# Output panels held back for the layer norm: two tiles finished first, and ScalarE rounding three weight panels

## The reference

```python
for layer in range(2):                      # first block; the second has no cross attention
    x = layer_norm(ALPHA * x + mixer(x) @ w_out, g0, b0)
    x = layer_norm(ALPHA * x + memory_cross_attention(x, mem, wq, wkv, wo), g1, b1)
    x = layer_norm(ALPHA * x + swiglu(x, w_gu, w_down), g2, b2)
```

## Time and profile before

| | us |
|---|---|
| median of 3 runs (3221.38 to 3228.93) | 3225.34 |
| the profiled execution | 3220.99 |
| its span, first to last instruction | 3219.2 |
| PE busy | 3025.5 |
| POOL busy | 1751.4 |
| DVE busy | 921.4 |
| ACT busy | 645.0 |

### The profile page before, as it was taken

How to read it: one execution, slowest core, us unless ns; L and a number is a source line. 1 busy time by engine, 2 the same in 40 slices (tenths; PEclk the granted TensorE clock), 3 DMA queues, 4 the chain that set the end, 5 groups by cost and what they waited for, 6 DMA issues and landing times.

```text
span 3219.2 us, 35940 instructions
## 1 busy us (share of the span) xinstructions
PE 3025.5 (94%) x15048; PEld 2511.7 (78%) x15048; DVE 921.4 (29%) x1470; ACT 645.0 (20%) x1330; POOL 1751.4 (54%) x1472
## 2 busy tenths in 40 slices
PE   7889999999999897999999999899999998999998
PEld 6776778888887666788888887878888886788887
DVE  3535402311023295023100221833110056530102
ACT  1224212211010162122100121452010032420100
POOL 5540383566665503836666656423666665556664
PEclk9999999999999998999999999989999999899999
DMA  4221241322223202412322232002323222033232
GB/s 143 71 74 40 70 143 50 105 92 98 99 87 104 66 1 66 144 53 92 105 92 94 90 112 92 1 1 81 103 92 104 93 98 79 14 100 97 92 105 79
DMA packets 182498, 267.15 MB, mean 83 GB/s; under 512 B 6592, under 2 KB 145984, under 8 KB 182336
## 3 DMA queue, kind: packets, MB, share of 16 engines
q1 hardware_dynamic: 174240, 243.28, 22.9%
q10 hardware_dynamic: 8096, 21.56, 2.0%
HBM read 262.73 MB, written 2.10 MB: 82 GB/s over the span
## 4 chain that ended last, share of the span: by engine, by line
PE 79%; DVE 14%; POOL 3%; issue 1%; ACT 1%; DMA 1%; ACTq 0%; DVEq 0%; POOLq 0%
PE PS L464 23%; PE PS L465 23%; PE PS L466 23%; PE PS L785 3%; POOL wlo L2084 2%; DVE PS L665 2%; DVE x_row L660 1%; PE PS L771 1%; DVE nmx L1434 1%; PE PS L1324 1%; DVE xT_lo L566 1%; DVE x_row L672 1%; PE PS L917 1%; POOL whi L2079 1%; PE PS L549 1%
## 5 line engine op out<-in xcount | busy, mean ns | idle before, releaser
L2079 POOL TENSOR_SCALAR whi<-raw 128x1024 fp32r<-128x1024 f32 x460 | 485.7, 1076 | 1336.2 <-DMA raw<-ffn_w 270.0
L2084 POOL TENSOR_TENSOR wlo<-raw,whi 128x512 fp32r<-128x512 f32 x920 | 1188.5, 1328 | 0.0
L464 PE MATMUL PS<-xT_hi,whi 128*128 128x512 f32 (+1 forms) x2304 | 856.0, 372 | 41.4 <-DVE xT_lo L566 29.1
L465 PE MATMUL PS<-xT_lo,whi 128*128 128x512 f32 (+1 forms) x2304 | 848.7, 368 | 0.0
L466 PE MATMUL PS<-xT_hi,wlo 128*128 128x512 f32 (+1 forms) x2304 | 848.5, 368 | 0.0
L464 PEld LDWEIGHTS PS<-xT_hi,whi 128*128 128x128 f32 x2304 | 441.6, 192 | 118.1 <-DVE xT_lo L566 32.4
L465 PEld LDWEIGHTS PS<-xT_lo,whi 128*128 128x128 f32 x2304 | 441.6, 192 | 71.5 <-issue 2.4
L466 PEld LDWEIGHTS PS<-xT_hi,wlo 128*128 128x128 f32 x2304 | 441.4, 192 | 70.1
L464 PE MATMUL PS<-whi,xT_hi 128*128 128x512 f32 x672 | 264.5, 394 | 23.6 <-ACT a_pre L1025 16.3
L960 DVE TENSOR_TENSOR htmp<-sil,PS 128x512 f32<-128x512 f32 x88 | 56.5, 683 | 804.0 <-ACT sil L945 804.0
L464 PE MATMUL PS<-whi,h_hi 128*128 128x512 f32 x704 | 274.1, 389 | 0.0
(11 more groups left out here) (360 smaller groups left out, 3218.5 us busy)
## 6 DMA issues: line engine op xcount, KB each, us to landing
raw<-ffn_w SPq DMA_DIRECT2D x66, 1024.0 KB, 5.0
raw<-ffn_w_gu SPq DMA_DIRECT2D x44, 1024.0 KB, 5.1
raw<-ffn_w_down SPq DMA_DIRECT2D x22, 1024.0 KB, 5.0
raw<-mem_wkv SPq DMA_DIRECT2D x16, 1024.0 KB, 5.4
raw<-even_w_in SPq DMA_DIRECT2D x14, 1024.0 KB, 5.2
raw<-ev_w_in SPq DMA_DIRECT2D x14, 1024.0 KB, 5.3
raw<-odd_w_in SPq DMA_DIRECT2D x12, 1024.0 KB, 5.1
raw<-od_w_in SPq DMA_DIRECT2D x10, 1024.0 KB, 5.0
```

Source lines behind the costliest of these rows:

```text
L464: pe.matmul(o, lhs[0], rhs[0], start=start, stop=False, skip_group_check=True)
L465: pe.matmul(o, lhs[0], rhs[1], start=False, stop=False, skip_group_check=True)
L2079: pool.tensor_scalar(whi[b][:, cs], raw[b][:, cs], 1.0, 1.0, ALU.mult, ALU.mult).then_inc(panel_hi, 1)
L2084: m = pool.tensor_tensor(wlo[b][:, cs], raw[b][:, cs], whi[b][:, cs].bitcast(F32), ALU.subtract)
```

## The change

Three panels are held instead of two. In each of the ten stages PE adds N-2, N-1 and N to tiles 0 and 1 first, then does tiles 2 and 3, with the transposes of tiles 0 and 1 in between. The orders of ACT and DVE around the norm follow: both tiles' transposes are copied before tile 2 is centred. The hi halves of the panels N, N+1 and N+2 are made by ACT (`act_cut`), not by POOL; POOL keeps their lo halves and waits for ACT through `panel_hi_act`.

```diff
         for st in stages:
...
+            last_panel.append(len(panels) + nk // 2 - 1)
+        cut_panels = [n + k for n in last_panel for k in range(3) if n + k < len(panels)]
+
+        def act_cut(act, n):
+            b = n % NB
+            act.wait_ge(panel_loaded[b], 16 * (n // NB + 1))
+            for q in range(2):
+                cs = slice(1024 * q, 1024 * q + 1024)
+                act.activation(whi[b][:, cs], raw[b][:, cs], ACT.Copy).then_inc(panel_hi_act, 1)
...
-            for i in range(nk // 2 - 2):
+            for i in range(nk // 2 - 3):
...
             def finish(t):
-                add(1, t).then_inc(y_ready, 1)
-            two = next_panel(pe)
-            for t in (0, 1, 2):
-                add(0, t)
-            two += next_panel(pe)
+                add(2, t).then_inc(y_ready, 1)
+            three = next_panel(pe)
+            add(0, 0)
+            add(0, 1)
+            three += next_panel(pe)
+            add(1, 0)
+            add(1, 1)
+            three += next_panel(pe)
             finish(0)
             finish(1)
+            add(0, 2)
             add(0, 3).then_inc(panel_used, 1)
-            finish(2)
             if head:
                 turn(0)
+            add(1, 2)
+            if head:
+                turn(1)
+            add(1, 3).then_inc(panel_used, 1)
+            finish(2)
             finish(3)
             if head:
-                turn(1)
                 head(pe, lambda: (turn(2), turn(3)))
...
+            last = last_panel[at_stage[0]]
+            act_cut(act, last)
             deviation(0)
             deviation(1)
             if head:
                 act_turn(act, xT_hi, 0, KD, 0, 0)
+                act_turn(act, xT_hi, 0, KD, 2, 1)
+                act_cut(act, last + 1)
             deviation(2)
             if head:
-                act_turn(act, xT_hi, 0, KD, 2, 1)
+                act_cut(act, last + 2)
             deviation(3)
...
             finish(0)
             finish(1)
-            centre(2)
             if head:
                 dve_turn(dve, xT_hi, xT_lo, 0, KD, 0, 0)
-            else:
+                dve_turn(dve, xT_hi, xT_lo, 0, KD, 2, 1)
+            centre(2)
+            if not head:
                 finish(2)
             centre(3)
             if head:
-                dve_turn(dve, xT_hi, xT_lo, 0, KD, 2, 1)
                 finish(2)
             finish(3)
...
-                for q in range(2):
+                by_act = n in cut_panels
+                for q in range(0 if by_act else 2):
                     cs = slice(1024 * q, 1024 * q + 1024)
                     pool.tensor_scalar(whi[b][:, cs], raw[b][:, cs], 1.0, 1.0, ALU.mult, ALU.mult).then_inc(panel_hi, 1)
...
+                    if q % 2 == 0 and by_act:
+                        pool.wait_ge(panel_hi_act, 2 * cut_panels.index(n) + q // 2 + 1)
```

More of the change, by code:

```diff
@@ L267, in build @@
         panel_hi = sem("panel_hi")
+        panel_hi_act = sem("panel_hi_act")
         panel_split = sem("panel_split")
@@ L375, in build @@
         pool_at = []
+        last_panel = []
         for st in stages:
@@ L569, in dve_turn @@
             m.then_inc(lo_ready, 1)
+        cut_panels = [n + k for n in last_panel for k in range(3) if n + k < len(panels)]
+        def act_cut(act, n):
+            assert n in cut_panels
+            b = n % NB
[3 more added lines that the diff above has]
+                act.activation(whi[b][:, cs], raw[b][:, cs], ACT.Copy).then_inc(panel_hi_act, 1)
         n_ln = {"pe": 0, "act": 0, "dve": 0}
@@ L596, in add @@
                 ts = slice(128 * t, 128 * t + 128)
-                h, lo = two[i]
+                h, lo = three[i]
                 for c in range(2):
@@ L600, in add @@
                         cs = slice(1024 * k + 512 * c, 1024 * k + 512 * c + 512)
-                        kk = nk - 4 + 2 * i + k
+                        kk = nk - 6 + 2 * i + k
                         m = product(pe, PS[:, 2 * t + c, :], (lh[:, kk, ts], ll[:, kk, ts]),
-                                    (h[:, cs], lo[:, cs]), False, i == 1 and k == 1)
+                                    (h[:, cs], lo[:, cs]), False, i == 2 and k == 1)
                 return m
             def finish(t):
-                add(1, t).then_inc(y_ready, 1)
-            two = next_panel(pe)
-            for t in (0, 1, 2):
-                add(0, t)
-            two += next_panel(pe)
+                add(2, t).then_inc(y_ready, 1)
[6 more added lines that the diff above has]
+            three += next_panel(pe)
             finish(0)
             finish(1)
+            add(0, 2)
             add(0, 3).then_inc(panel_used, 1)
-            finish(2)
             if head:
                 turn(0)
+            add(1, 2)
[3 more added lines that the diff above has]
+            finish(2)
             finish(3)
             if head:
-                turn(1)
                 head(pe, lambda: (turn(2), turn(3)))
@@ L2081, in _ @@
                     cs = slice(512 * q, 512 * q + 512)
-                    if q % 2 == 0:
-                        pool.wait_ge(panel_hi, 2 * n + q // 2 + 1)
+                    if q % 2 == 0 and by_act:
+                        pool.wait_ge(panel_hi_act, 2 * cut_panels.index(n) + q // 2 + 1)
+                    elif q % 2 == 0:
+                        pool.wait_ge(panel_hi, 2 * (n - sum(k < n for k in cut_panels)) + q // 2 + 1)
                     m = pool.tensor_tensor(wlo[b][:, cs], raw[b][:, cs], whi[b][:, cs].bitcast(F32), ALU.subtract)
```

## The result

The changed kernel takes 3198.47 us (median of 4, 3197.73 to 3204.66) against 3224.67 for the one before in the same comparison: ratio 0.9922, 95% interval 0.9905 to 0.9939, 26 us faster. Forecast were 3193 (range 3177 to 3216), 32 us faster. The profiled execution's span is 3196.8.

What follows compares the result with a forecast made beforehand. PE's waits were taken to bound the kernel, 4.1 to 4.5 us per norm for xT_lo. Terms 28.0 + 5.2 - 0.4 = 33 us off the profiled 3220.99 give 3188; counted from the median 3225.3, 3193 (range 3177 to 3216).

Steps and rivals of the forecast that it cites:

- the three waits: PE's new waits at a norm: for N 0.6 us, N+1 0.1 at the head's start, N+2 1.7 48 matmuls later.
- The copies on ScalarE: ACT's copy of the first 1024 columns of a panel's hi half, taken as 1.1 us before POOL can start.
- POOL beside L665: POOL's lo half of N+2 takes 5.96 us, not 5.05, because tile 3's centring on DVE runs beside it.
- The seven norms before an FFN or mixer: Transposes of tiles 2 and 3 start 3.6 us earlier per norm: 25.2, with the longer slow stretches 28.0 us gained.
- three longer stretches: Three of the seven norms had a longer 1.2 GHz stretch at the head; its going gives 1.2 + 1.0 + 0.6 us more.
- rival A: The new wait for N+2 brings a slow-clock stretch each time, 1.7 us at nine norms, 15 us lost: 3208; chance 0.18.
- The two cross attentions: At the norms before them POOL's chain through the memory's panels counts and ends 2.6 us earlier, twice: 5.2 us gained.
- The last norm: Nothing follows it; N's wait of 0.6 us is paid and 0.2 comes back: a loss of 0.4 us.
- Rival C: With a fast ACT copy and POOL not slowed, N+2 is ready in time, 12 us more gained: 3181; chance 0.13.
- B: Slower: as rival A, but N's wait also brings a slow stretch and N+2's a double one: 3238; chance 0.05.
- D: Tile 0's row and N+1 miss their slack and waits inside the mixers take back half the gain: 3209 to 3220; chance 0.12.
- the slack that was forecast: Tile 0's row is ready 0.8 us before PE transposes that tile in the second norm, so PE does not wait.

Runs made afterwards that it cites:

- the last kernel: Two panels held with tiles 0 and 1 first, as in the run with two held, but ScalarE makes N+2's hi half alone, in four pieces: 3173.23 us, ratio 0.9846.

## Why the prediction was right

**That the panels take the norm's place: right.** The wait for the lo parts went at every norm; the forecast named the three waits and put them at 0.6, 0.1 and 1.7 us. Measured in the second norm: 0.53, none and 1.74, the last between 1.73 and 1.74 at all nine norms. The two one-sided runs (order alone, ScalarE alone) show that with three panels held both parts are needed, which the forecast had only in its arithmetic.

**The copies on ScalarE: right in size.** 1.1 us was taken between bounds of 0.63 and 1.27; the group's mean is 1.05.

```profile
L584 ACT ACTIVATE whi<-raw 128x1024 fp32r<-128x1024 f32 x56 | 56.1, 1051 | 447.1 <-DMA raw<-ffn_w_down 178.6 <-DMA raw<-ffn_w 178.5 <-DMA raw<-mem_wo 29.8
```

The estimate from the Trainium skill's page "ScalarE: Activation LUTs" (section "What ACT_TABLE_LOAD costs"), 1.04 us, agrees.

**POOL beside L665: right.** 5.96 us was taken for N+2's lo half, 6.00 measured. That is 0.96 more than the 5.04 of an undisturbed lo half, so the 0.9 of the forecast held and not the 1.29 that it set beside it; N+1's lo half wasn't disturbed at all (5.04). What was not in the sum is that DVE pays too: its L691 took 2.19 us there instead of 1.29. This is off the path: tile 3's row ended at 585.25 and the transposes of tiles 2 and 3 start at 588.99.

**The seven norms before an FFN or mixer: the term was 28.0 and gave 22.3.** This is the term that was mis-sized. (By the forecast's own figures the first of its three longer stretches gives 1.1, not 1.2.) Two things were off. (a) 0.3 to 0.6 us a norm, but for the one before the odd mixer, in the steps between N and the head. At the second norm, from N's load to the transposes of tiles 2 and 3 the forecast had 45.15 us (540.55 to 585.7), measured 45.73 (543.26 to 588.99). Of this 0.6, 0.1 is that N is ready 0.1 later after its load's issue (the wait itself is shorter than forecast, since PE wants N later too), 0.4 that the matmuls and transposes from there to the head take 23.73 us, not 23.36, and 0.1 the head up to the transposes. Before the odd mixer nothing is missing, since a later wait there, for a transfer of the mixer, also fell, from 1.31 to 0.89 us. (b) The slow clock in two of the seven, some 1.5 us each, which is rival A in part.

**Rival A.** The forecast gave 18% to a slow stretch at every norm and counted none in its own number; the truth lies between. In two profiles of the changed kernel it comes in 9 of 18. Its price was set too high: the forecast took 1.7 us at nine norms, but before a cross attention the window is 83.5 us with a stretch and 83.4 without (odd to cross, the second and the first profile), since POOL's chain sets it. Seven norms can lose by it. Two of them did in the first profile, some 3 us, and four in the second, some 6 us (56.5 to 57.8 us, and 56.3 to 58.1). In the order-only kernel, with waits of 1.9 to 2.9 us and a gain of 1.3 us at the undisturbed second norm, the stretches and the longer waits for N together eat the whole gain. In the two kernels with two panels held, whose waits are at most 1.65 us, no head has one.

The trace of before already held both outcomes for one length of wait. The two waits of PE in 224 to 262 us were 2.13 us each; the forecast named the one that was followed by a slow stretch (241.8) and not the other, which ended at 228.7:

```profile
228.00:232.00 4.00, 3.30 (x18) 2.34 (x19) 1.91 (x7) 1.14 (x4) 0.00 (x0) 1.00 0.00 0
```

The Trainium skill ("TensorE: Matmul & The Clock Gate", "HAM oscillation — how this bites in real kernels") tells of a loop that waits 3 to 5 us for data in each turn and starts every turn slow. The old waits of 4.15 to 4.52 us agree, 9 of 9; of the waits of 1.73 to 1.85 us only half were followed by a stretch.

**The two cross attentions: 5.2 forecast, 5.1 measured** (2.3 and 2.8). That POOL's chain through the memory's panels sets it fits the five waits of PE that are left after the change (415 to 450 us before, the same panels after):

```profile
PE PS L467 <- POOL wlo L2113: 5.5, 5, 1.3
```

**The last norm: 0.4 forecast, 0.3 measured.**

**Sum.** 33 forecast for the profiled execution; 27.1 in the norms, less 4.8 for the rest of the span, 22.4 in this profile; 26.2 between the medians. The mechanism was right, and what was off are sizes: (a) and the clock, some 3 us each in this profile. That the forecast 3193 lies only 5.5 us below the median, inside the range, is partly luck: it counts no slow stretch, and how many come differs from profile to profile (three and six). Rival C (N+2 in time), B and D are out: the wait for N+2 was there at every norm, and tile 0's row (ended at 564.83) was there 0.8 us before its transposes (565.67), the slack that was forecast. For D, that the gain would be lost again inside the mixers can't be told from one profile, as their lengths vary by more; in the FFNs between the norms it is kept whole: each takes 310.43 us in every profile.

**What stays open.** Why the clock falls behind one wait of 1.74 us and not behind the next is not settled; the 2.86 us wait in the second norm of the order-only kernel brought no slow stretch either. That holding three panels has no use of its own follows from the run with two held: its norm windows are shorter in sum (590.1 us, without ScalarE) than those of every kernel tried that holds three (591.1 at best, with ScalarE). Other orders with three held were not tried. What would remain to gain in the memory phases was not tried.

## What to carry to other kernels

When an order is changed to end some tiles earlier, write down for every buffer when it is freed and when its next content is wanted: here the change freed N+1's buffer 11.7 us later than before (22.6 us after the issue of N's load, not 10.9) and paid for it with waits that an order with one panel less held does not have. Ask how few buffers the new order needs before adding an engine to hide their lateness. On a path that TensorE sets, a wait costs 1.3 to 1.8 us more than its length when one stretch at half clock of 3.4 us follows it (the windows above, waits of 1.7 to 4.5 us), so shortening a wait can gain more than the time taken off it. Where another engine sets the path, as before the cross attentions here, the stretch cost almost nothing.

## What the runs showed of the hardware

- A wait of 1.73 to 1.85 us of TensorE was followed by a stretch of 3.4 us at 1.2 GHz in 9 of 18 cases, those of 1.9 to 2.9 us in the order-only kernel in 5 of 9 (once for 6.8 us). The old wait of 4.15 to 4.52 had one in 9 of 9 (three times for 6.8 us), and so had the 3.9 us of the run with ScalarE's part alone (four times for 6.8 us). Waits up to 1.65 us had none in the norm windows; four of 1.4 to 2.0 us behind late loads had none either. Two waits of 2.13 us in the trace of before differ too. Length alone doesn't decide it.
- DVE's centring with two inputs in SBUF and POOL's splitting slow each other in the same stretch: the centring took 2.19 us instead of 1.29 (up to 2.45 in the last kernel), POOL's lo half 6.00 instead of 5.04, and 6.47 where it met two centrings. POOL's hi half suffers too (2.07 to 2.87). With ScalarE's part alone, where POOL stood still meanwhile, all 40 centrings took 1.29.
- A 1 MB load lands after 5.0 us in the median (5.6 for the memory's keys and values). In every profile 3 to 9 of the 227 loads behind the first three took 6.1 us or more, the longest 8.2; two of them are the same panels in all nine profiles. Where the late panel was on the path it came through as PE's wait: 1.4 to 2.0 us for N+2 with the buffers freed sooner, 2.4 for N in the order-only kernel. Where it wasn't, as for N in the last kernel (6.29 us), PE didn't wait.
